# Delta-rule recurrence: both key operands as one 128-column stationary, U and the transposed values stacked over the partitions

## The reference, cut to what matters

```python
def _rwkv7_scan(r, w, k, v, kh, a):
...
    def step(state, inp):
        r_t, w_t, k_t, v_t, kh_t, a_t = inp
        removed = jnp.einsum('zhvk,zhk->zhv', state, kh_t)
        state = (state * w_t[:, :, None, :] - removed[..., None] * (kh_t * a_t)[:, :, None, :]
                 + v_t[..., None] * k_t[:, :, None, :])
        return state, jnp.einsum('zhvk,zhk->zhv', state, r_t)
```

## Time and profile before

| | |
|---|---|
| median of 3 runs | 2000.55 us (1999.71 to 2002.95) |
| profiled execution, its own time | 1998.48 us |
| its span in the profile | 1996.8 us |
| mean granted TensorE clock | 0.994 |
| PE (matmul) busy | 1957.4 us, 98% |
| DVE / ACT busy | 57% / 24% |

### The profile page before, as it was taken

One profiled execution on the slowest core, in us unless ns is written; L12 is line 12 of the kernel. 1 busy time (PEld: TensorE's weight loads), 2 busy tenths in 40 slices (PEclk: granted clock), 3 DMA queues, 4 the chain that ended last, 5 costly groups with the idle time before them and its releaser, 6 DMA issues.

```text
span 1996.8 us, 36120 instructions
## 1 busy us (share of the span) xinstructions
PE 1957.4 (98%) x14899; PEld 1357.2 (68%) x14899; DVE 1128.3 (57%) x1898; ACT 469.8 (24%) x904; POOL 249.3 (12%) x234
## 2 busy tenths in 40 slices
PE   8999999999999999999999999899999999999997
PEld 6778979964878979994445565899985444444443
DVE  2697486753569557665578846545447433233324
ACT  3164110001436201000331144433323101110111
POOL 4684000000567100000000001000000000000000
PEclk9999999999999999999999999999998999999999
DMA  8333545454533355536722234200011999999995
GB/s 259 127 127 106 211 151 169 146 200 124 187 127 127 113 212 161 169 127 242 266 85 84 85 127 169 87 3 3 4 48 71 385 428 429 427 429 428 428 428 225
DMA packets 138857, 385.55 MB, mean 193 GB/s; under 512 B 16953, under 2 KB 64417, under 8 KB 127589
## 3 DMA queue, kind: packets, MB, share of 16 engines
q1 hardware_dynamic: 138725, 383.61, 51.2%
HBM read 382.55 MB, written 1.05 MB: 192 GB/s over the span
## 4 chain that ended last, share of the span: by engine, by line
PE 81%; DMA 8%; DVE 7%; ACT 2%; issue 1%; SPq 0%; POOL 0%; DVEq 0%; ACTq 0%; POOLq 0%
PE psum L706 13%; PE psum L411 11%; PE psum L1726 9%; PE psum L2470 8%; DMA arena<-in_ex_up_dram 8%; PE psum L3318 7%; PE psum L748 5%; PE psum L431 3%; PE psum L602 3%; PE psum L3343 2%; PE psum L667 2%; PE psum L764 2%; PE psum L3248 2%; PE psum L682 1%; PE psum L2894 1%; PE psum L1931 1%
## 5 line engine op out<-in xcount | busy, mean ns | idle before, releaser
L411 PE MATMUL psum<-arena,ring 128*128 128x256 f32 x1472 | 326.1, 380 | 0.0
L411 PEld LDWEIGHTS psum<-arena,ring 128*128 128x128 f32 x1472 | 276.0, 189 | 46.1 <-issue 7.2
L2470 PE MATMUL psum<-arena 64*64 64x64 f32 (+1 forms) x4320 | 180.8, 238 | 6.2 <-DVE arena L2695 3.5
L2470 PEld LDWEIGHTS psum<-arena 64*64 64x64 f32 x4320 | 172.5, 135 | 8.5 <-DVE arena L2695 3.6
L706 PE MATMUL psum<-arena,ring 128*128 128x128 f32 x1280 | 149.5, 275 | 0.0
L706 PEld LDWEIGHTS psum<-arena,ring 128*128 128x128 f32 x1280 | 146.1, 192 | 0.0
L1726 PE MATMUL psum<-arena,ring 128*128 128x512 f32 (+2 forms) x432 | 142.0, 490 | 0.0
L815 ACT ACTIVATE arena<-psum 128x512 f32<-128x512 f32 (+2 forms) x80 | 42.0, 544 | 350.3 <-PE psum L411 121.6
L1726 PEld LDWEIGHTS psum<-arena,ring 128*128 128x128 f32 (+1 forms) x432 | 81.1, 188 | 60.7 <-issue 55.4
L706 PE MATMUL psum<-arena 128*128 128x128 f32 x960 | 113.7, 274 | 0.0
L706 PEld LDWEIGHTS psum<-arena 128*128 128x128 f32 x960 | 110.4, 192 | 0.0
(11 more groups left out here) (505 smaller groups left out, 3108.5 us busy)
## 6 DMA issues: line engine op xcount, KB each, us to landing
ring<-in_w_in_dram SPq DMA_DIRECT2D x29, 2048.0 KB, 8.1
ring<-in_ffn_w_dram SPq DMA_DIRECT2D x46, 1024.0 KB, 7.7
arena<-in_ex_gate_dram SPq DMA_DIRECT2D x15, 2048.0 KB, 17.0
arena<-in_ex_up_dram SPq DMA_DIRECT2D x15, 2048.0 KB, 21.5
arena<-in_ex_down_dram SPq DMA_DIRECT2D x15, 2048.0 KB, 22.0
ring<-in_ex_gate_dram SPq DMA_DIRECT2D x14, 2048.0 KB, 14.3
ring<-in_ex_up_dram SPq DMA_DIRECT2D x14, 2048.0 KB, 18.7
ring<-in_ex_down_dram SPq DMA_DIRECT2D x14, 2048.0 KB, 20.6
```

Source lines behind the costliest of these rows:

```text
L411: ins = pe.matmul(bank[:, j, :], w[:, kc, c * P:(c + 1) * P], moving[:, kc, :], start=kc == 0, stop=kc == k - 1)
L2470: ins = pe.matmul(bank[r, u, :], a[r, u], b[r, u], start=i == 0, stop=i == len(terms) - 1)
```

## The change

The stationaries b and k of one head are laid next to each other, so that one matmul with a stationary of 64 partitions and 128 columns gives both products ("mn", one bank for each head r; k first for one head and b first for the other). The halves land in the two halves of the partitions. "t1" is made in the same way. The transposed values of one head and its U go to opposite halves of the partitions (`K.uv`; for one of the two heads in a free slot of the weight ring), so that "y" and "st" have one matmul with 128 contraction partitions and 64 columns in place of the two terms in U and in the values; the term in the state stays as a 64 by 64 matmul. VectorE has "mn" masks for each r in place of "mr" and "nr", a further operation in `hats` for 64 partitions (a second copy of k for the first head), and the start of the inverse in two halves. ScalarE copies "wu" in three operations in place of one, "t1" in two of 256 columns in place of one of 512, and the transposed values in two halves.

```diff
@@ wkv_tensor
     def each(key, n, *terms):
...
         for u in range(HP):
             for i, (a, b) in enumerate(terms):
-                for r in HEAD_ROWS:
-                    ins = pe.matmul(bank[r, u, :], a[r, u], b[r, u], start=i == 0, stop=i == len(terms) - 1)
+                for r in range(2):
+                    ins = pe.matmul(bank[HEAD_ROWS[r], u, :], a(r, u), b(r, u), start=i == 0, stop=i == len(terms) - 1)
...
-        each(("mr", c, z), 2, (t.b, kr))
+        for r in range(2):
+            pe.wait_ge(K.empty(("mn", r, c, z)), K.empty_count(("mn", r, c, z)))
+        for u in range(HP):
+            for r in range(2):
+                ins = pe.matmul(by_two(K.bank(("mn", r, c, z)))[:, u], t.keys(r, u), kr[HEAD_ROWS[r], u], start=True, stop=True)
...
-        each(("nr", c, z), 2, (t.k, kr))
...
-        for i, src in enumerate((t.b, t.k)):
-            for u in range(HP):
-                for r in HEAD_ROWS:
-                    ins = pe.matmul(bank[r, u, i, :], src[r, u, :], one[r, :], start=True, stop=True)
+        for u in range(HP):
+            for r, key in enumerate(keys):
+                ins = pe.matmul(by_pair(K.bank(key), CH)[:, u, :], t.keys(r, u), one[HEAD_ROWS[r], :], start=True, stop=True)
...
         if c >= LAT:
-            each(("y", c, z), 1, (u0, t.own(c, RB)), (vt, t.nk[:, :, 1 + c % 2, :]), (t.s, t.gr[:, :, 0, :]))
+            each(("y", c, z), 1, (uv, lambda r, u: t.both(c, r)[:, u, READ, :]), (at_head(t.s), at_head(t.gr[:, :, 0, :])))
         if c < CHUNKS - 1:
-            terms = [(t.own(c, KT), vt), (t.own(c, BT), u0)]
+            terms = [(lambda r, u: t.both(c, r)[:, u, TURNED, :], uv)]
             if c > 0:
-                terms += [(t.gr[:, :, 1, :], t.s)]
+                terms += [(at_head(t.gr[:, :, 1, :]), at_head(t.s))]
             each(("st", c, z), 1, *terms)
@@ wkv_vector, hats
-        tt_op(t.kb, K.k_and_a[:, :, :, at:at + CH], t.p_inv.unsqueeze(1).broadcast_to([P, 2, HP, CH]), ALU.mult).then_inc(K.sem["hats"], 1)
+        tt_op(t.kbk[:, :, 0:2, :].rearrange("p u i t -> p i u t"), K.k_and_a[:, :, :, at:at + CH],
+              t.p_inv.unsqueeze(1).broadcast_to([P, 2, HP, CH]), ALU.mult)
+        first = HEAD_ROWS[0]
+        tt_op(t.kbk[first, :, 2, :], K.kmod[first, :, at:at + CH], t.p_inv[first], ALU.mult).then_inc(K.sem["hats"], 1)
...
+        for r, rows in enumerate(HEAD_ROWS):
+            ins = tt_op(t.inv[rows], t.both(c, r)[rows, :, STRICT, :], K.one[rows].unsqueeze(1).broadcast_to([HD, HP, CH]), ALU.add)
```

More of the change, by code:

```diff
@@ L1569, in wkv_groups @@
             if LAT <= c < CHUNKS:
-                keys += [("t1", c, z)]
+                keys += [("t1", r, c, z) for r in range(2)]
             if c > LAT:
@@ L2510, in values_turned @@
             for u in range(HP):
-                for r in HEAD_ROWS:
-                    ins = pe.matmul(bank[r, u, j, :], K.rv[r, u, at:at + CH], one[r, :], start=True, stop=True)
+                for r in range(2):
+                    ins = pe.matmul(bank[HEAD_ROWS[1 - r], u, j, :], K.rv[HEAD_ROWS[r], u, at:at + CH], one[HEAD_ROWS[r], :],
+                                    start=True, stop=True)
         ins.then_inc(K.full(key), 1)
@@ L2537, in level @@
                 for u in range(HP):
-                    for r in HEAD_ROWS:
-                        ins = pe.matmul(bank[r, u, i, :], a[r, u], b[r, u], start=True, stop=True)
+                    for r in range(2):
+                        ins = pe.matmul(bank[HEAD_ROWS[r], u, i, :], a(r, u), b(r, u), start=True, stop=True)
             ins.then_inc(K.full(key), 1)
@@ L2644, in wkv_scalar @@
     for i in range(CHUNKS // 2):
-        copy(("vt", i), K.rv[:, :, 2 * i * CH:2 * (i + 1) * CH], by_pair(K.bank(("vt", i)), 2 * CH))
+        key, cols = ("vt", i), slice(2 * i * CH, 2 * (i + 1) * CH)
+        act.wait_ge(K.full(key), K.full_count(key))
+        for r in range(2):
+            rows = HEAD_ROWS[1 - r]
+            ins = act.activation(K.uv[r][rows, :, cols], by_pair(K.bank(key), 2 * CH)[rows], ACT.Copy)
+        ins.then_inc(K.empty(key), 1)
     for c in range(CHUNKS):
@@ L2700, in inner @@
         n = 2 if lat else 1
-        key = ("mr", c, z)
-        dve.wait_ge(K.full(key), K.full_count(key))
-        ins = tt_op(t.strict_out(c, lat), by_two(K.bank(key))[:, :, 0:n, :], spread(K.masks[:, z, 0:n, :]), ALU.mult)
-        ins.then_inc(K.empty(key) if lat else K.sem["strict"], 1)
+        for r in range(2):
+            key = ("mn", r, c, z)
+            dve.wait_ge(K.full(key), K.full_count(key))
+            tt_op(t.both(c, r)[:, :, 0:n, :], by_two(K.bank(key))[:, :, 0:n, :], spread(K.masks[:, z, 0:n, :]), ALU.mult).then_inc(
+                K.empty(key) if lat else K.sem["strict"], 1)
         dve.wait_ge(K.full(("m", c, z)), K.full_count(("m", c, z)))
@@ L2708, in inner @@
         if lat:
-            dve.wait_ge(K.empty(key), K.drained_count(key))
+            for r in range(2):
+                dve.wait_ge(K.empty(("mn", r, c, z)), K.drained_count(("mn", r, c, z)))
         else:
             dve.wait_ge(K.sem["strict"], strict_of(c, z) - 1)
-        tt_op(t.inv, t.powers(0)[:, :, 0, :], spread(K.one), ALU.add).then_inc(K.sem["inv_start"], 1)
-    def pairs(c, z):
-        t, lat = K.wkv[z], c >= LAT
-        n = 2 if lat else 1
-        key = ("nr", c, z)
-        dve.wait_ge(K.full(key), K.full_count(key))
-        ins = tt_op(t.pairs_out(c, lat), by_two(K.bank(key))[:, :, 0:n, :], spread(K.masks[:, z, 0:n, :]), ALU.mult)
-        ins.then_inc(K.empty(key) if lat else K.sem["pairs"], 1)
+        for r, rows in enumerate(HEAD_ROWS):
+            ins = tt_op(t.inv[rows], t.both(c, r)[rows, :, STRICT, :], K.one[rows].unsqueeze(1).broadcast_to([HD, HP, CH]), ALU.add)
+        ins.then_inc(K.sem["inv_start"], 1)
     def moved(c, z):
@@ L2774, in wkv_vector @@
                 moved(c - 1, z)
-        if c < CHUNKS:
-            for z in range(ZS):
-                pairs(c, z)
         if c > 0:
@@ L3629, in __call__ @@
         return view
-ARENA = 40736
+ARENA = 40840
 def layer_tiles(K, tile):
@@ L3820, in second_tiles @@
     top, tile.at = tile.at, rest
-    K.wkv = [Wkv(tile) for _ in range(ZS)]
+    grown = split(flat(K.mixed[:, 4:, :]), ZS)
+    K.wkv = [Wkv(tile, grown[:, z, :].rearrange("p (u n t) -> p u n t", u=HP, n=2)) for z in range(ZS)]
+    used = [K.ring.at["wo2", hf][0] for hf in range(2)]
+    spare = next(i for i in range(SLOTS) if i not in used)
+    K.uv = [K.slot[:, spare, 0:HP * S_ALL].rearrange("p (u t) -> p u t", u=HP), K.rv]
     tile.at = max(tile.at, top)
```

115 lines of the change are left out of this document (57 added, 58 removed).

## The result

The changed kernel takes 2006.58 us (median of 8 executions, 2005.03 to 2008.25), the kernel before 2000.13 us in the same comparison (8, 1998.44 to 2002.95). The ratio is 1.0032, with a 95% interval of 1.0022 to 1.0042: slower, by 6.4 us where 10.4 were forecast.

What follows compares the result with a forecast made beforehand. TensorE, busy nearly throughout the recurrence, was taken as the bound. Saved steps -24.7, form changes +31.5 and VectorE +3.6 us gave +10.4 us, hence 2011.0 us, in a range of 2002 to 2022.

Steps and rivals of the forecast that it cites:

- Rival 2: TensorE in "y" and "st": changes between 64*64 and 128*64 are free, so faster, 1987.9 us; chance 0.12.
- Rival 3: TensorE's form changes: only the 0.09 us pause is paid, the next load being hidden; no difference, 2000.3 us; chance 0.09.
- Rival 4: TensorE's granted clock falls as "y" and "st" stream with pauses; 11 us more, 2022 us; chance 0.14.
- The saved steps: Fewer TensorE steps in "mn" (13.9 us), "y" and "st" (10.3) and "t1" (0.5): 24.7 us saved.
- the changes: TensorE's changes of stationary form: 24 wide at 0.20 us and 178 narrow at 0.15, 31.5 us added.
- VectorE, 3.6 us: The extra operation in `hats` delays `grow` and the levels TensorE waits for: 3.6 us added, bounds 0 and 5.
- nv: Product now using two off-diagonal array quarters; pauses there might cost up to 4.8 us, left out of the sum.

Runs made afterwards that it cites:

- experiment 1: Changed kernel with "y" and "st" issuing the stacked terms of all four pairs first, then their state terms: 1988.60 us, ratio 0.9940 to the kernel before.
- experiment 3: Changed kernel with VectorE's added second copy of k moved from between the levels to behind the sixth level's `grow`: 2003.50 us, ratio 1.0016 to the kernel before.
- experiment 2: Changed kernel with "nv" reading the same half of the partitions that it writes (values then differ from the reference): 2038.24 us; recurrence 231.0 us against 228.2.
- experiment 8: Changed kernel with each "mn" and "t1" matmul split into two of 64 by 64, in four array quarters: 1997.25 us, ratio 0.9983 to the kernel before.
- experiments 5 to 7: Changed kernel with products grouped by form, adding in turn: second k late, "nv" between level 1's matmuls, inverse started later: 1979.66, 1977.94, 1973.50 us.

## Why the prediction was right, and what was off

- **The sign and the mechanism held.** The pauses at changes of form outweigh the saved steps. The forecast was 2011.0 us in a range of 2002 to 2022; it is 2006.58.
- **Rival 2 (changes between 64\*64 and 128\*64 are free, 1987.9 us) falls.** They cost 0.15 us each, in the profile and in experiment 1.
- **Rival 3 (only 0.09 us each) falls.** The load of a new form starts only with its group, as the earlier trace rows had it.
- **Rival 4 (the clock falls) falls.** "y" and "st" run at the full granted clock. The stretch's mean of 0.99 comes from 3.41 us at half clock at its start, ahead of any "y" or "st", and the kernel before has the same.
- **The saved steps, 24.7 us, and the changes, 31.5 us,** stand where they can be read: 2.99 us for "mn", "m" and "gr" for 2.97 by my terms (24 x 0.109 + 0.35), 4.12 us for "y" and "st" for the 4.2 forecast.
- **VectorE, 3.6 us,** is 3.1, by the medians of experiment 3 and by its chunks. The part that was too large is the latent chunks': 0.45 for 0.6 in each of chunks 3 to 6. The others held, with 0.33 for 0.3 in chunks 0 to 2.
- **The term that was mis-sized is "nv".** I wrote that should the array pause at the off-diagonal quarters it would cost up to 4.8 us, and left it out of the sum. It costs nothing and gives 2.8 us (experiment 2), 0.36 us a chunk, since those quarters work beside the diagonal ones for three steps at either end. The bound had only one side; the other, that two tiles without a common quarter overlap, could have been drawn from the earlier trace rows, where two halves of the array stream side by side.
- **The sum again:** -24.7 + 31.5 + 3.1 - 2.9 = +7.0 us. With the 0.143 us for a narrow change that the chunks of experiment 1 give, in place of 0.15, it is 178 x 0.007 = 1.2 us less, +5.8. The stretch with the first `hats` has +6.3 and the medians +6.4, between the two.

## What to carry to other kernels

Count the changes of the stationary's form before the steps that it saves: here a change costs some 0.15 to 0.20 us, as much as about three steps of 64 columns, and the stacked operand paid only once its products stood together. With operands of 64 rows and columns, the four quarters of the array can be filled without changing form, by writing one product of a pair into the other half of the partitions. And a bound drawn for an unknown cost needs its gaining side too.

## What the runs showed of the hardware

- A change of the stationary's form between 64\*64 and 128\*64 (f32) costs 0.15 us by the distance of starts and 0.143 by the chunks of experiment 1, though only the contraction rows differ. From 64\*64 into 64\*128 and back again ("mn") costs 0.37 us together; that 0.20 of this is the way in rests on the earlier trace rows and isn't shown by itself.
- Four 64 by 64 quarters work at once: 32 records of 128 moving columns in 0.87 us (experiment 8), where "mr" and "nr", two quarters at a time, took 1.74 before. Entering the crossing quarters from the straight ones has no pause; records of both stand interleaved at 1408.94 to 1409.11 in the changed kernel.
- VectorE takes 0.41 us for 64 partitions by 256 elements (L2708) and 0.42 for 128 partitions by as many (L2694 of the earlier trace rows).
- The granted clock fell in stretches that differ from one execution to another: 0.57 from 1185.5 to 1189.5 us in the changed kernel's, behind 2.02 us in which TensorE stood idle, and none there in the profile of before, with the same idle time. At the recurrence it was 0.50 for 3.41 us right behind 3.81 us of idle TensorE in the changed kernel's, and for 10.24 us ahead of the recurrence, with TensorE busy, in experiment 3's. Spans and stretches of single profiles therefore differ by a few microseconds whatever the edit, and experiments 5 to 7, whose steps are 2 to 7 us, can't be sized by their totals alone.
